# New memory for the W_o stage, a weight home that does not overlap it, and an earlier tenth weight load

## The chip, the cores and the metric

One core of one Trainium2 chip runs the whole program. The metric is the device time of one execution in microseconds. Three runs of the kernel before took 1180.64, 1182.9 and 1184.21 us; the median is 1182.9 us.

## The reference

One layer of a hybrid decoder for 512 prompt tokens and 8 sample tokens (520 rows of 1024 numbers, f32). Three gated branches (dilated attention, a state-space layer, cross-attention) are merged, multiplied by W_o and added to x. A mixture of experts follows:

```
h  = x + merged @ w_o                     # 520 x 1024
hn = rmsnorm(h, norm2)
grp_logits = hn @ w_grp + b_grp           # 4 groups, the best one
exp_logits = hn @ w_exp + b_exp           # 32 experts, the best two of the group
y  = sum over the two experts e of gate_e * ((silu(hn @ w1[e]) * (hn @ w3[e])) @ w2[e])
out = rmsnorm(h + y, norm_f)
```

Each of w1[e], w3[e] and w2[e] has 2 MB. The 96 of them are 201 MB and are read once. The change touches the stage from `h` to the first expert.

## The kernel before, in words

**Weight homes.** On-chip memory is one array, `arena`; a place in it is given in KB per partition. A weight matrix takes 16 KB per partition. `HOMES` lists ten such places. Load number n (n = 3 e + part; part 0 is w1, 1 is w3, 2 is w2 of expert e) goes to home n mod 10. The first ten loads wait only until other uses of their place are over. From load 10 on, `wait_release` waits until TensorE has used up load n - 10: semaphores `w1x` (w1), `gu` (w3), `y` (w2). So load 10 waits for expert 0's w1 product, load 15 for expert 1's w2 product. All weight loads are issued by SP, in order, into one hardware queue. SP also issues the loads of x for the W_o stage, between weight loads.

**The W_o stage.** The 520 rows are five tiles in the order `ORDER = (4, 0, 1, 2, 3)`: tile i = 0 is the 8 sample rows, tiles 1 to 4 have 128 rows each. For a tile, in the order in which its parts depend on each other:

- PE (TensorE): `out_rows(i, quarter)`, four quarters of 8 matmuls of 128x512 each (L1171). Quarters 0 and 1 make the left half of the product, 2 and 3 the right half.
- DVE (VectorE): `add_half(i, half)` adds the product onto x in `xh` (L2096).
- ACT (ScalarE): squares of the left half (L1612) and of the right half (L1619), a square root, then `hn` = x times the reciprocal, written to `hnb` (L1627).
- POOL (GpSimd): stores the tile's h rows to memory (L707, semaphore `hacc`) and then its hn rows (L709, semaphore `hnst`), both in one software queue.
- PE: `turn_half` transposes h, `router(i)` makes the logits.
- DVE: `first_squares(i)` waits for the left squares of tile i. After it in DVE's program comes `route(i - 1)`, some 20 small operations (L2129 the first, L2143 sets `chosen`) that pick the experts of the tile before, and then `add_half(i, 1)`.
- PE: `rank(i - 1)` (L1203, L1205) needs `chosen` of tile i - 1. It stands behind quarter 3 of tile i and ahead of the first quarter of tile i + 1, and each engine runs its program in order.

After the last tile PE makes the index lists (`idxmm`), DVE turns them into integers (L2190), and POOL gathers 128 rows of hn for the first two experts (L721). It waits for the lists and for all `hnst` and `hacc` stores.

**Memory of that stage, before.** `xh` has three buffers and `hnb` two; the unneeded squares go to `scrap`. W_o lies in two pieces of 16 KB, at 50 (home 6) and at 187.25 (home 8). Home 7 is where `gates`, the left operand of the product, lies. So loads 6, 7 and 8 wait for the stage's end. SP's order there is: two W_o loads, the last of norm_f's loads (`gain_f`), three x tiles, load 0; after the merge load 1; then, each time behind `hacc`, `hn` and `ht` of an earlier tile, an x tile and loads 2, 3, 4, and an x tile and load 5. Load 6 follows the last product. Load 7 is issued in two halves, one behind the `hnst` stores and one, like loads 8 and 9, behind the first gather (`xg`).

Of the kernel before, what the change touches and what calls it, by code (L numbers as in the profile page):

```python
# [32 lines left out]
P = 128  # L33
# [64 lines left out]
HOMES = (66, 107.25, 123.25, 139.25, 155.25, 171.25, 50, 91.25, 187.25, 30)  # L98
# [5 lines left out]
SPLIT = tuple(16 if i == 7 else 0 for i in range(NHOME))  # L104
# [32 lines left out]
def build(nc, t):  # L137

    with ExitStack() as ctx:
# [165 lines left out]
        scrap = [at(87, D // 2), at(89, D // 2)]  # L305
# [35 lines left out]
        hT = [at(XN + 16, 2, P), at(86, 2, P)]  # L341
        xg = at(82, D)
        gain_f = at(46, D)
# [4 lines left out]
        y_end = at(87, D // 2)  # L348
        pick_end = [at(MK + 16.25, NT, CAP), at(MK + 18.25, NT, CAP)]
        place_end = at(89, TOK)  # L350
# [22 lines left out]
        rows_in = [sem(f"s_rows_in{i}") for i in range(3)]  # L373
        hacc = [sem(f"s_hacc{i}") for i in range(3)]
        hnst = [sem(f"s_hnst{i}") for i in range(2)]

        def h_back_in(T):

            return (rows_in[T], 16 * (len(range(T, NT, 3)) + 1)) if T < 3 else \
                (kdec[T], 32 * len(range(T, NB, NSLOT)) + 16)  # L380
# [3 lines left out]
                    ssm_right=("ssmp", 16), pick=("Sfree", KT), turned=("Sj", KT), placed=("merged", KT), sums=("Pj", 2 * KT),  # L384
# [75 lines left out]
        def _(sp):  # L460
# [21 lines left out]
            def load_x(i):  # L482
                T = ORDER[i]
                src = t["x_prompt"].rearrange("(a r) c -> r a c", r=NCLS)[T] if T < 4 else t["x_sample"]
                sp.dma_start(xh[i % 3][0:ROWS[T], :], src).then_inc(rows_in[i % 3], 16)
# [86 lines left out]
            split = home(2, 1)[0]  # L572

            def load_half(k0):
                sp.dma_start(up_w[split][:, k0:k0 + KT // 2, :],
                             t["w3"][2].rearrange("(p k) f -> p k f", p=P)[:, k0:k0 + KT // 2, :]
                             ).then_inc(wld[split], 16)
# [16 lines left out]

            sp.wait_ge(s["npass"], 1)
# [21 lines left out]
        def _(pool):  # L617
# [86 lines left out]
            for i, T in enumerate(ORDER):  # L704
                n = ROWS[T]
                pool.wait_ge(s["h"], 2 * i + 2)
                pool.dma_start(h_acc[T * P:T * P + n, :], xh[i % 3][0:n, :]).then_inc(hacc[i % 3], 16)  # L707
                pool.wait_ge(s["hn"], i + 1)
                pool.dma_start(t["hn_dram"][T * P:T * P + n, :], hnb[i % 2][0:n, :]).then_inc(hnst[i % 2], 16)  # L709
            pool.wait_ge(s["xgclear"], 1)  # L710
            for i in range(2):
                pool.wait_ge(hnst[i], 16 * len(range(i, NT, 2)))
            for i in range(3):
                pool.wait_ge(hacc[i], 16 * len(range(i, NT, 3)))
# [47 lines left out]
        def _(pe):  # L762
# [404 lines left out]
            def out_rows(i, quarter):  # L1167

                T, half = ORDER[i], quarter // 2
                for k in range(4 * (quarter % 2), 4 * (quarter % 2) + 4):  # L1170
                    last = pe.matmul(bank[:, 2 * (i % 2) + half, :], gates[:, k, T * P:T * P + P],  # L1171
                                     w_o[k // 4][:, k % 4, half * 512:(half + 1) * 512],
                                     start=k == 0, stop=k == KT - 1)
                if quarter % 2 == 1:
                    last.then_inc(s["wo_mm"], 1)

            def turn_half(i, half):
                n = ROWS[ORDER[i]]
                pe.wait_ge(s["h"], 2 * i + half + 1)
                if half:  # L1180
                    pe.wait_ge(s["htA"], i + 1)
                else:
                    wait_from(pe, s["htD"], i)
                for k in range(4):
                    last = pe.transpose(bank[:, 4, k * P:k * P + n],
                                        xh[i % 3][0:n, (4 * half + k) * P:(4 * half + k + 1) * P], ident[0:n, 0:n])
                last.then_inc(s["ht"], 1)
# [30 lines left out]
            pe.wait_ge(s["wo"], 32)  # L1218
            pe.wait_ge(s["Sfree"], KT)
            for k in range(KT):  # L1220
                pe.wait_ge(s["merged"], k + 1)
                for q in range(4):
                    last = pe.matmul(bank[32 * q:32 * q + NB, 0, 0:256], gates[:, k, SEQ:TOK],
                                     w_o[k // 4][:, k % 4, q * 256:(q + 1) * 256],
                                     start=k == 0, stop=k == KT - 1, skip_group_check=True)
# [41 lines left out]
            def one_pass(p, again):  # L1267
# [30 lines left out]
                def up(e):  # L1298
                    u = e % 2
                    pe.wait_ge(s["xc"], p * NE + (2 * (e // 2) + 4))  # L1300
                    pe.wait_ge(s["hid"], p * NE + (e + 1))
                    for part, done in enumerate(("w1x", "gu")):
                        i, turn = home(e, part)
                        w = up_w[i]
                        pe.wait_ge(wld[i], p * (16 * LOADS[i]) + (16 * turn + 16 + SPLIT[i]))
# [16 lines left out]
                def down(e):  # L1322
# [6 lines left out]
                    pe.wait_ge(wld[i], p * (16 * LOADS[i]) + (16 * turn + 16 + SPLIT[i]))  # L1329
# [73 lines left out]
        def _(act):  # L1403
# [202 lines left out]
            for q in range(1, 4):  # L1606
                act.activation(hnb[0][0:NB, q * 256:(q + 1) * 256], bank[32 * q:32 * q + NB, 0, 0:256], ACT.Copy
                               ).then_inc(s["h_moved"], 1)
            for i, T in enumerate(ORDER):
                n, x = ROWS[T], xh[i % 3]  # L1610
                act.wait_ge(s["h"], 2 * i + 1)
                act.activation(scrap[0][0:n, :], x[0:n, 0:512], ACT.Square, accum_out=stat[0:n, 32 + i:33 + i]  # L1612
# [6 lines left out]
                act.activation(scrap[1][0:n, :], x[0:n, 512:D], ACT.Square, accum_out=stat[0:n, 37 + i:38 + i]  # L1619
# [6 lines left out]
                wait_from(act, hnst[i % 2], 16 * (i // 2))  # L1626
                act.activation(hnb[i % 2][0:n, :], x[0:n, :], ACT.Copy, scale=stat[0:n, 5 + i:6 + i]  # L1627
# [8 lines left out]
            act.activation(scrap[0][:, 0:1], scrap[0][:, 0:1], ACT.Silu).then_inc(s["hss"], 1)  # L1636
# [64 lines left out]
        def _(dve):  # L1701
# [388 lines left out]
            def add_half(i, half):  # L2090
                cols = slice(512 * half, 512 * half + 512)
                dve.wait_ge(s["wo_mm"], 2 * i + half)
                if half == 0:
                    dve.wait_ge(rows_in[i % 3], 16 * (i // 3 + 1))
                x = xh[i % 3][:, cols]
# [8 lines left out]
            def turned_half(i):  # L2104
# [4 lines left out]
                                bank[:, 4, :].rearrange("p (k a) -> p k a", k=4)[:, :, 0:n]).then_inc(s["htD"], 1)  # L2109
# [57 lines left out]
            TT(xh[0][0:NB, 256:D], xh[0][0:NB, 256:D], hnb[0][0:NB, 256:D], ALU.add).then_inc(s["vchain"], 1)  # L2167
# [104 lines left out]
            dve.wait_ge(hnst[1], 16 * len(range(1, NT, 2)))  # L2272
# [167 lines left out]
```

## Time and profile before

| what | value |
|---|---|
| median of three runs | 1182.9 us |
| profiled execution, its own time | 1183.2 us |
| its span (first to last instruction) | 1181.5 us |
| PE busy | 1066.9 us, 90% |
| DVE, ACT, POOL busy | 412.2, 227.1, 135.1 us |
| weight loads in the page's list of DMA issues | 95 of 2048 KB and 2 of 1024 KB |

The page cuts the span into 40 slices of 29.5 us. In slices 24 to 38 the DMA engines are 90% busy or more and move about 420 GB/s (392 in the second of them); in the five slices before, from 561 to 709 us, they move 34, 313, 169, 173 and 412 GB/s. A busy TensorE is not a TensorE at its peak; idle time counts only on the engine that others wait for.

### The profile page before, as it was taken

How to read it: one execution, taken by the hardware profiler on the slowest of the kernel's cores; microseconds unless marked ns; L12 is line 12 of the kernel's file. 1: busy time of each engine (PE TensorE's matmuls, PEld its weight loads, DVE VectorE, ACT ScalarE, POOL GpSimd, SP SyncE). 2: the span in 40 equal slices, each digit the busy share in tenths (PEclk: the TensorE clock that was granted, in tenths of full speed). 3: DMA queues.
4: the chain of work that ended last, by engine and by line, in shares of the span. 5: the costliest groups of instructions: out<-in, count | busy, mean ns of one | idle time of the engine just before them, and what ended most of it. 6: DMA issues, size and time to landing. Idle time of an engine off the chain costs nothing.

```text
span 1181.5 us, 16647 instructions
## 1 busy us (share of the span) xinstructions
PE 1066.9 (90%) x6831; PEld 761.1 (64%) x6831; DVE 412.2 (35%) x869; ACT 227.1 (19%) x445; POOL 135.1 (11%) x153
## 2 busy tenths in 40 slices
PE   7999999999999999999999599987887787888885
PEld 6888888887888888878845355544444444444441
DVE  3993305926566655422543510100000000000003
ACT  4103021125232222410032201111101111111114
POOL 2113401003010100000010011110011111110100
PEclk9999999999999999999999799999999999999998
DMA  6771266434766645279084499999999999999974
GB/s 229 248 263 55 90 226 229 136 113 169 231 227 229 219 158 188 93 280 395 34 313 169 173 412 392 415 418 420 417 418 421 420 420 421 424 421 419 418 316 148
DMA packets 50812, 330.32 MB, mean 280 GB/s; under 512 B 9084, under 2 KB 12236, under 8 KB 37552
## 3 DMA queue, kind: packets, MB, share of 16 engines
q1 hardware_dynamic: 33760, 259.75, 54.9%
q0 software_dynamic: 15104, 63.85, 16.3%
q10 hardware_dynamic: 1872, 5.66, 1.3%
q8 instruction: 53, 0.87, 0.3%
q14 instruction: 23, 0.19, 0.0%
HBM read 319.18 MB, written 62.11 MB: 323 GB/s over the span
## 4 chain that ended last, share of the span: by engine, by line
PE 64%; DMA 31%; ACT 2%; issue 1%; DVE 1%; SPq 1%; POOLq 0%; ACTq 0%; DVEq 0%
DMA arena<-in_w 26%; PE bank L777 14%; PE bank L957 12%; PE bank L1308 8%; PE bank L1171 5%; PE bank L1333 4%; PE bank L1162 4%; DMA arena<-in_w_stream 2%; PE bank L1081 2%; PE bank L869 2%; PE bank L790 1%; PE bank L948 1%; PE bank L996 1%; PE bank L1017 1%; ACT arena L1588 1%
## 5 line engine op out<-in xcount | busy, mean ns | idle before, releaser
L1308 PE MATMUL bank<-arena 128*64 128x256 f32 x2048 | 261.3, 411 | 64.9 <-DMA arena<-in_w 64.8
L1308 PEld LDWEIGHTS bank<-arena 128*64 128x64 f32 x2048 | 160.2, 143 | 157.9 <-issue 51.0
L777 PE MATMUL bank<-arena 128*128 128x260 f32 x768 | 169.8, 383 | 0.6 <-DMA arena<-in_w_stream 0.6
L777 PEld LDWEIGHTS bank<-arena 128*128 128x128 f32 x768 | 145.5, 190 | 23.3 <-issue 1.0
L957 PE MATMUL bank<-arena 128*128 128x260 f32 x672 | 152.6, 384 | 1.7 <-DVE arena L1913 1.7
L957 PEld LDWEIGHTS bank<-arena 128*128 128x128 f32 x672 | 125.7, 190 | 22.0 <-DVE arena L1913 2.5
L2244 DVE TENSOR_TENSOR arena<-arena,bank 128x256 f32<-128x256 f32 x32 | 13.5, 421 | 326.7 <-ACT arena L1645 326.7
L1333 PE MATMUL bank<-arena 128*64 128x512 f32 x512 | 117.2, 600 | 3.9 <-DVE arena L2250 3.0
L733 POOL DMA_INDIRECT y_dram<-arena,scatter_rows x31 | 44.3, 1428 | 385.6 <-ACT arena L1661 355.2
L1333 PEld LDWEIGHTS bank<-arena 128*64 128x64 f32 x512 | 37.3, 138 | 64.9 <-issue 55.6
L1645 ACT ACTIVATE arena<-bank 128x256 f32<-128x256 f32 x32 | 12.3, 383 | 318.9 <-PE bank L1308 318.9
L1661 ACT ACTIVATE arena<-bank,arena 64x512 f32<-64x512 f32 x62 | 42.3, 682 | 105.8 <-PE bank L1333 100.1
L1171 PE MATMUL bank<-arena 128*128 128x512 f32 x128 | 58.7, 601 | 0.0
L1438 ACT ACTIVATE arena<-bank 128x520 f32 (+1 forms) x24 | 14.5, 603 | 150.4 <-PE bank L777 150.4
L2236 DVE TENSOR_TENSOR arena<-bank,arena 128x512 f32<-128x512 f32 x32 | 20.6, 686 | 62.1 <-PE bank L1295 62.1
L1162 PE MATMUL bank<-arena 128*128 128x260 f32 x192 | 42.2, 382 | 0.0
L1162 PEld LDWEIGHTS bank<-arena 128*128 128x128 f32 x192 | 36.5, 190 | 5.6
L1171 PEld LDWEIGHTS bank<-arena 128*128 128x128 f32 x128 | 23.1, 190 | 23.6 <-issue 23.4
L2023 DVE TENSOR_TENSOR arena<-arena,bank 128x520 f32<-128x520 f32 x24 | 16.6, 692 | 54.7 <-PE bank L1081 26.5
L1774 DVE TENSOR_TENSOR arena<-arena 128x16 f32<-128x16 f32 (+6 forms) x24 | 13.0, 583 | 60.3 <-ACT arena L1478 59.8
L1081 PE MATMUL bank<-arena 128*128 128x260 f32 x128 | 29.7, 387 | 0.6 <-DVE arena L2023 0.6
L633 POOL DMA_DIRECT2D out_sample_swa_k<-in_cache_swa_k x24 | 14.0, 582 | 138.5 <-PE bank L777 69.5
(356 smaller groups left out, 1123.8 us busy)
## 6 DMA issues: line engine op xcount, KB each, us to landing
arena<-in_w SPq DMA_DIRECT2D x95, 2048.0 KB, 35.7
arena<-in_w_stream SPq DMA_DIRECT2D x50, 512.0 KB, 5.1
out_sample_swa_k<-in_cache_swa_k POOLq DMA_DIRECT2D x8, 2047.0 KB, 9.6
out_sample_swa_v<-in_cache_swa_v POOLq DMA_DIRECT2D x8, 2047.0 KB, 10.0
arena<-in_cache_mem_v SPq DMA_DIRECT2D x8, 512.0 KB, 8.2
arena<-in_w_o SPq DMA_DIRECT2D x2, 2048.0 KB, 9.9
out_sample_swa_k<-in_cache_swa_k POOLq DMA_DIRECT2D x8, 511.0 KB, 5.9
out_sample_swa_v<-in_cache_swa_v POOLq DMA_DIRECT2D x8, 511.0 KB, 5.7
```

What stands on the lines that cost most here:

```text
L733: pool.indirect_dma_start(out=h_acc, out_offset=bass.IndirectOffsetOnAxis(ap=rows, axis=0), in_=y_sb[e % NYS], in_offset=None, bounds_chec ...
L777: last = pe.matmul(bank[:, 2 * u + h, 0:HALF], ring[u][:, k, :], x[:, k, h * HALF:(h + 1) * HALF], start=k == 0, stop=k == KT - 1)
L869: last = pe.matmul(bank[:, 2 * u, 0:MEM], ring[u][:, k, :], memn[:, k, :], start=k == 0, stop=k == KT - 1)
L957: last = pe.matmul(bank[:, product_bank[m], 0:HALF], wq[i][left[m]][:, k, :], right[m][:, k, :], start=opens and k == 0, stop=k == 3, skip ...
L1081: last = pe.matmul(bank[:, SSM_BANK[j] + h, 0:HALF], w_ssm[k][:, j * P:(j + 1) * P], ssmT[:, k, h * HALF:(h + 1) * HALF], start=k == 0, st ...
L1162: last = pe.matmul(bank[:, 2 + 2 * i + h, 0:HALF], w[:, k, j * P:(j + 1) * P], src[:, k, h * HALF:(h + 1) * HALF], start=k == 0, stop=k == ...
L1171: last = pe.matmul(bank[:, 2 * (i % 2) + half, :], gates[:, k, T * P:T * P + P], w_o[k // 4][:, k % 4, half * 512:(half + 1) * 512], start ...
L1308: last = pe.matmul(bank[64 * q:64 * q + CAP, 2 + u, part * FE // 2:(part + 1) * FE // 2], xgT[e // 2 % 2][:, k, 64 * u:64 * u + CAP], w[:, ...
L1333: last = pe.matmul(bank[64 * q:64 * q + CAP, 6 + u, :], hT[u][:, j, par_ * CAP:(par_ + 1) * CAP], down_w[i][:, j, par_, q * 512:(q + 1) * ...
L1661: last = act.activation(y_sb[v][:, q * 512:(q + 1) * 512], bank[half, 6 + u, :], ACT.Copy, scale=slot_gate[half, e:e + 1])
L2023: return TT(g, g, bank[:, b0:b0 + 2, 0:HALF], ALU.mult)
L2236: TT(xgT[pair % 2][:, 4 * half:4 * half + 4, :], bank[:, half, :].rearrange("p (k a) -> p k a", k=4), wide(gain2_x[:, 4 * half:4 * half + ...
```

## The change

Homes 0, 6, 7 and 8 move. W_o is cut in rows of 4 KB at 38, 42, 46 and 50.25 and one piece of 16 KB at 187.25 (now home 7). Home 6 is now at 75.25 and overlaps neither W_o nor `gates`, so load 6 need not wait for the stage's end. To make room, `xh` gets two buffers instead of three and `hnb` one instead of two; `scrap` is gone, and the squares are written into `hnb`, so the left squares of tile i wait for the `hnst` store of tile i - 1. In the last tile PE takes the lower half of W_o (k 4 to 7) first, for both halves of the product; behind that load 7 is issued, and loads 8 and 9 wait for the last product, the stores and `hn`, but not for the gather. norm_f's load moves behind the last weight load.

```diff
-HOMES = (66, 107.25, 123.25, 139.25, 155.25, 171.25, 50, 91.25, 187.25, 30)
+HOMES = (59.25, 107.25, 123.25, 139.25, 155.25, 171.25, 75.25, 187.25, 91.25, 30)
...
-        w_o = [at(HOMES[6], 4, D), at(HOMES[8], 4, D)]
-        xh = [at(30 + 4 * i, D) for i in range(3)]
-        hnb = [at(42, D), at(MK + 16.25, D)]
+        w_o = [at(kb, D) for kb in (38, 42, 46, 50.25)] + [at(HOMES[7] + 4 * k, D) for k in range(4)]
+        xh = [at(30 + 4 * i, D) for i in range(2)]
+        hnb = at(MK + 16.25, D)
...
-            sp.dma_start(w_o[1], t["w_o"][:, 4:8, :]).then_inc(s["wo"], 16)
             sp.wait_ge(s["Sj"], KT)
-            sp.dma_start(w_o[0], t["w_o"][:, 0:4, :]).then_inc(s["wo"], 16)
-            sp.dma_start(gain_f, t["norm_f"].partition_broadcast(P)).then_inc(s["gainf"], 16)
-            for i in range(3):
+            for k0, n in ((0, 2), (2, 1), (3, 1), (4, 4)):
...
+                sp.dma_start(dst, src).then_inc(s["wo"], 16)
+            for i in range(2):
                 load_x(i)
             load_weight(0, 0)
             sp.wait_ge(s["merged"], KT)
             load_weight(0, 1)
-            for i in (3, 4):
-                sp.wait_ge(hacc[i % 3], 16)
-                sp.wait_ge(s["hn"], i - 2)
-                sp.wait_ge(s["ht"], 2 * (i - 2))
+            for i in range(2, NT):
+                sp.wait_ge(hacc[i % 2], 16 * (i // 2))
+                sp.wait_ge(s["hn"], i - 1)
+                sp.wait_ge(s["ht"], 2 * (i - 1))
                 load_x(i)
-                for n in ((2, 3, 4), (5,))[i - 3]:
+                for n in ((2, 3), (4, 5), (6,))[i - 2]:
                     load_weight(n // 3, n % 3)
+            sp.wait_ge(*later("wo_right", 1))
+            load_weight(2, 1)
             sp.wait_ge(s["wo_mm"], 2 * NT - 1)
-            load_weight(2, 0)
+            load_weight(2, 2)
             for i in range(2):
-                sp.wait_ge(hnst[i], 16 * len(range(i, NT, 2)))
-            load_half(0)
-            for i in range(3):
-                sp.wait_ge(hacc[i], 16 * len(range(i, NT, 3)))
+                sp.wait_ge(hacc[i], 16 * len(range(i, NT, 2)))
             sp.wait_ge(s["ht"], 2 * NT)
-            sp.wait_ge(s["xg"], 16)
-            load_half(KT // 2)
-            load_weight(2, 2)
+            sp.wait_ge(s["hn"], NT)
             load_weight(3, 0)
             for n in range(NHOME, NLOAD):
                 wait_release(n // 3, n % 3)
                 load_weight(n // 3, n % 3)
+            sp.dma_start(gain_f, t["norm_f"].partition_broadcast(P)).then_inc(s["gainf"], 16)
...
             def out_rows(i, quarter):
...
+                if i == NT - 1:
+                    half, opens, closes = quarter % 2, quarter < 2, quarter >= 2
+                    ks = range(4, 8) if opens else range(4)
...
+                elif i == NT - 1 and quarter == 1:
+                    last.then_inc(later_sem("wo_right"), 1)
...
-                turn_half(i, 0)
+                if i < NT - 1:
+                    turn_half(i, 0)
                 slot_tokens(i - 2)
                 out_rows(i, 3)
+                if i == NT - 1:
+                    turn_half(i, 0)
                 rank(i - 1)
...
                 act.wait_ge(s["h"], 2 * i + 1)
-                act.activation(scrap[0][0:n, :], x[0:n, 0:512], ACT.Square, accum_out=stat[0:n, 32 + i:33 + i]
+                wait_from(act, hnst, 16 * i)
+                act.activation(hnb[0:n, 0:512], x[0:n, 0:512], ACT.Square, accum_out=stat[0:n, 32 + i:33 + i]
                                ).then_inc(s["hss"], 1)
...
-                wait_from(act, hnst[i % 2], 16 * (i // 2))
-                act.activation(hnb[i % 2][0:n, :], x[0:n, :], ACT.Copy, scale=stat[0:n, 5 + i:6 + i]
+                act.activation(hnb[0:n, :], x[0:n, :], ACT.Copy, scale=stat[0:n, 5 + i:6 + i]
```

In the last tile the second transposition uses another bank (2 instead of 4). The weight waits of PE lose the extra count of the split load.

## Rows read from the trace of the kernel before

**Rows 1.** Chain of waits, 760 to 1181 us: start, us, what
```profile
806.41 35.70 DMA arena<-in_w
```
**Rows 2.** Waits of PE, 684 to 780 us: us in total, times, longest
```profile
PE bank L1308 <- DMA arena<-in_w: 0.6, 1, 0.6
```
**Rows 3.** Timeline of SP, 520 to 760 us: start, us, line, what, count
```profile
601.79 0.33 SPq L485 DMA_DIRECT2D arena<-in_x_prompt  x1
...
718.01 0.80 SPq L466 DMA_DIRECT2D arena<-in_w  x2
```
**Rows 4.** Timeline of SP, 687 to 688 us
```profile
687.79 0.33 SPq L466 DMA_DIRECT2D arena<-in_w  x1
```
**Rows 5.** Chain of waits, 540 to 760 us
```profile
664.40 8.44 DMA hn_dram<-arena
...
673.78 5.08 DMA arena<-hn_dram,gather_rows
```
**Rows 6.** Timeline of POOL, 586 to 684 us; in brackets the idle time before
```profile
602.01 0.52 POOL L709 DMA_DIRECT2D hn_dram<-arena  x1 [6.21 <-ACT arena L1627]
...
615.02 0.54 POOL L709 DMA_DIRECT2D hn_dram<-arena  x1 [4.69 <-ACT arena L1627]
```
**Rows 7.** DMA issues at 602, 609.8 and 615 us: KB, us to landing
```profile
hn_dram<-arena POOLq DMA_DIRECT2D x1, 32.0 KB, 4.1
...
y_dram<-arena POOLq DMA_DIRECT2D x1, 512.0 KB, 11.6
...
hn_dram<-arena POOLq DMA_DIRECT2D x1, 512.0 KB, 9.2
```
**Rows 8.** DMA issues at 632.4, 664.4 and 681.8 us
```profile
hn_dram<-arena POOLq DMA_DIRECT2D x1, 512.0 KB, 2.9
...
hn_dram<-arena POOLq DMA_DIRECT2D x1, 512.0 KB, 8.4
...
arena<-hn_dram,gather_rows POOLq DMA_INDIRECT x1, 10.3
```
**Rows 9.** DMA issues of a weight load at 602.2 and at 718.0 us
```profile
arena<-in_w SPq DMA_DIRECT2D x1, 2048.0 KB, 8.3
...
arena<-in_w SPq DMA_DIRECT2D x1, 2048.0 KB, 10.9
```
**Rows 10.** Timeline of ACT, 586 to 684 us
```profile
616.95 0.63 ACT L1612 ACTIVATE arena<-arena 128x512 f32<-128x512 f32 x1 [2.21 <-DVE arena L2096]
```
**Rows 11.** Timeline of DVE, 586 to 684 us
```profile
618.00 0.26 DVE L2129 SCALAR_TENSOR_TENSOR arena<-bank,arena 128x36 f32<-128x36 f32 x1
...
621.66 0.19 DVE L2143 TENSOR_TENSOR arena<-arena 128x32 f32<-128x32 f32 x1
...
660.73 0.69 DVE L2096 TENSOR_TENSOR arena<-arena,bank 128x512 f32<-128x512 f32 x1 [3.59 <-PE bank L1171]
...
670.36 0.38 DVE L2190 TENSOR_SCALAR gather_rows<-bank 64x16 uint32<-64x16 f32 x2 [0.74 <-PE bank L1212]
```
**Rows 12.** Timeline of PE, 586 to 684 us
```profile
608.39 0.41 PE L1205 MATMUL bank<-arena 128*128 128x32 f32 x2
...
625.81 0.39 PE L1205 MATMUL bank<-arena 128*128 128x32 f32 x2
...
652.52 3.68 PE L1171 MATMUL bank<-arena 128*128 128x512 f32 x8
```
**Rows 13.** Timeline of PE, 795 to 860 us: one wait of an expert
```profile
810.46 9.20 PE L1308 MATMUL bank<-arena 128*64 128x256 f32 x64 [3.68 <-DMA arena<-in_w]
```
**Rows 14.** Stretch of 4 us: PE, PEld, DVE, ACT, POOL busy, granted clock, DMA, GB/s
```profile
811.00:815.00 4.00, 4.00 (x24) 2.64 (x22) 0.00 (x0) 0.00 (x0) 0.00 (x0) 0.57 1.00 397
```
**Rows 15.** Page, DMA rate in 40 slices; and queues: packets, MB, share
```profile
GB/s 229 248 263 55 90 226 229 136 113 169 231 227 229 219 158 188 93 280 395 34 313 169 173 412 392 415 418 420 417 418 421 420 420 421 424 421 419 418 316 148
...
q1 hardware_dynamic: 33760, 259.75, 54.9%
q0 software_dynamic: 15104, 63.85, 16.3%
```

More of the change, by code:

```diff
@@ L103 @@
 END_BANK = (0, 2, 4, 6, 0)
-SPLIT = tuple(16 if i == 7 else 0 for i in range(NHOME))
 LATE = 29
@@ L372, in build @@
         wld = [sem(f"s_wld{i}") for i in range(NHOME)]
-        rows_in = [sem(f"s_rows_in{i}") for i in range(3)]
-        hacc = [sem(f"s_hacc{i}") for i in range(3)]
-        hnst = [sem(f"s_hnst{i}") for i in range(2)]
+        rows_in = [sem(f"s_rows_in{i}") for i in range(2)]
+        hacc = [sem(f"s_hacc{i}") for i in range(2)]
+        hnst = sem("s_hnst")
         def h_back_in(T):
-            return (rows_in[T], 16 * (len(range(T, NT, 3)) + 1)) if T < 3 else \
+            return (rows_in[T], 16 * (len(range(T, NT, 2)) + 1)) if T < 2 else \
                 (kdec[T], 32 * len(range(T, NB, NSLOT)) + 16)
@@ L706, in _ @@
                 pool.wait_ge(s["h"], 2 * i + 2)
-                pool.dma_start(h_acc[T * P:T * P + n, :], xh[i % 3][0:n, :]).then_inc(hacc[i % 3], 16)
+                pool.dma_start(h_acc[T * P:T * P + n, :], xh[i % 2][0:n, :]).then_inc(hacc[i % 2], 16)
                 pool.wait_ge(s["hn"], i + 1)
-                pool.dma_start(t["hn_dram"][T * P:T * P + n, :], hnb[i % 2][0:n, :]).then_inc(hnst[i % 2], 16)
+                pool.dma_start(t["hn_dram"][T * P:T * P + n, :], hnb[0:n, :]).then_inc(hnst, 16)
             pool.wait_ge(s["xgclear"], 1)
+            pool.wait_ge(hnst, 16 * NT)
             for i in range(2):
-                pool.wait_ge(hnst[i], 16 * len(range(i, NT, 2)))
-            for i in range(3):
-                pool.wait_ge(hacc[i], 16 * len(range(i, NT, 3)))
+                pool.wait_ge(hacc[i], 16 * len(range(i, NT, 2)))
             def one_pass(p, late=0):
@@ L1169, in out_rows @@
                 T, half = ORDER[i], quarter // 2
-                for k in range(4 * (quarter % 2), 4 * (quarter % 2) + 4):
+                ks = list(range(4 * (quarter % 2), 4 * (quarter % 2) + 4))
+                opens, closes = quarter % 2 == 0, quarter % 2 == 1
+                if i == NT - 1:
+                    half, opens, closes = quarter % 2, quarter < 2, quarter >= 2
+                    ks = range(4, 8) if opens else range(4)
+                for k in ks:
                     last = pe.matmul(bank[:, 2 * (i % 2) + half, :], gates[:, k, T * P:T * P + P],
-                                     w_o[k // 4][:, k % 4, half * 512:(half + 1) * 512],
-                                     start=k == 0, stop=k == KT - 1)
-                if quarter % 2 == 1:
+                                     w_o[k][:, half * 512:(half + 1) * 512],
+                                     start=opens and k == ks[0], stop=closes and k == ks[-1])
+                if closes:
                     last.then_inc(s["wo_mm"], 1)
+                elif i == NT - 1 and quarter == 1:
+                    last.then_inc(later_sem("wo_right"), 1)
             def turn_half(i, half):
@@ L1179, in turn_half @@
                 pe.wait_ge(s["h"], 2 * i + half + 1)
-                if half:
+                b = 2 if half and i == NT - 1 else 4
+                if half and b == 4:
                     pe.wait_ge(s["htA"], i + 1)
@@ L1184, in turn_half @@
                 for k in range(4):
-                    last = pe.transpose(bank[:, 4, k * P:k * P + n],
-                                        xh[i % 3][0:n, (4 * half + k) * P:(4 * half + k + 1) * P], ident[0:n, 0:n])
+                    last = pe.transpose(bank[:, b, k * P:k * P + n],
+                                        xh[i % 2][0:n, (4 * half + k) * P:(4 * half + k + 1) * P], ident[0:n, 0:n])
                 last.then_inc(s["ht"], 1)
@@ L1304, in up @@
                         w = up_w[i]
-                        pe.wait_ge(wld[i], p * (16 * LOADS[i]) + (16 * turn + 16 + SPLIT[i]))
+                        pe.wait_ge(wld[i], p * (16 * LOADS[i]) + (16 * turn + 16))
                         for k in range(KT):
@@ L1328, in down @@
                         pe.wait_ge(s["sgate"], p + 1)
-                    pe.wait_ge(wld[i], p * (16 * LOADS[i]) + (16 * turn + 16 + SPLIT[i]))
+                    pe.wait_ge(wld[i], p * (16 * LOADS[i]) + (16 * turn + 16))
                     for j in range(2):
@@ L1618, in _ @@
                 act.wait_ge(s["h"], 2 * i + 2)
-                act.activation(scrap[1][0:n, :], x[0:n, 512:D], ACT.Square, accum_out=stat[0:n, 37 + i:38 + i]
+                act.activation(hnb[0:n, 512:D], x[0:n, 512:D], ACT.Square, accum_out=stat[0:n, 37 + i:38 + i]
                                ).then_inc(s["hss"], 1)
@@ L1635, in _ @@
             act.wait_ge(s["hss"], 3 * NT)
-            act.activation(scrap[0][:, 0:1], scrap[0][:, 0:1], ACT.Silu).then_inc(s["hss"], 1)
+            act.activation(stat[:, 63:64], eps_ap, ACT.Silu).then_inc(s["hss"], 1)
             def one_pass(p, late=0):
@@ L2271, in _ @@
             slot_tables()
-            dve.wait_ge(hnst[1], 16 * len(range(1, NT, 2)))
+            dve.wait_ge(hnst, 16 * NT)
             for k in range(2):
```

39 lines of the change are left out of this document (18 added, 21 removed).

## The prediction

> **What bounds the kernel now.** I read the page's DMA rates first, then the chain of waits, then each engine's timeline around the W_o stage, and last the landing times of single transfers.
>
> The page shows two regimes. From some 690 us to the end of the weights the DMA rate stays close to 420 GB/s [rows 15], and the chain runs through weight transfers of some 36 us each, with short pieces of TensorE between [rows 1]. There the kernel is bound by the weight stream: what ends earlier is whatever lets the stream run earlier. Just before, it moves 34 to 313 GB/s [rows 15]: that is the room the change wants to fill, with loads 6 to 9.
>
> The reader is then to ask what releases the stream's later parts. Load 10 is issued at 687.8 [rows 4], when TensorE has finished w1 of expert 0. Load 15 is issued at 718.0 [rows 3], when expert 1's w2 product is done. In between, PE waits for weights for only 0.6 us in all [rows 2]. So from the first gather to load 15 TensorE sets the pace, not the weights. The gather is released by the last hn store (landed at 664.4 + 8.4 = 672.8) and takes 5.1 us, to 678.9 [rows 5]. Everything that moves the gather moves load 15, and from there the stream is full.
>
> **The change part by part.**
>
> *Loads 6 to 9 earlier.* Behind the first gather (678.9) now stand the second half of load 7 and loads 8 and 9. The plain count says that these two and a half vanish from the stream. But loads 10 to 14 follow TensorE's releases, and load 15 comes 30.2 us after load 10 (718.0 - 687.8). What can be gained is only the queue in front of load 15: it lands 10.9 us after its issue, a load with an idle queue in front lands after 8.3 [rows 9]. Five loads in 30 us leave the engines idle before load 15 in the new kernel. Gain 2.6 us. Bounds: nothing, if load 15 still finds a queue, and 2.6.
>
> *One hn buffer: the left squares wait for the store.* The squares of tile i now wait until the hn store of tile i - 1 has landed. Behind the squares stand `first_squares(i)`, `route(i - 1)` on DVE, and `rank(i - 1)` on PE, with tile i + 1's product behind that in PE's program. In tile 2 the squares start at 616.95 [rows 10], `route` at 618.00, its `chosen` ends at 621.85 [rows 11]. So `rank` can run 4.9 us after the squares begin; with two semaphore hops of 0.05 and 0.1 us it is 5.05 us after the landing.
>
> - Tile 0's store (32 KB) is issued at 602.0 [rows 6] and lands after 4.1 us [rows 7], because the x tile and two weight loads are issued from 601.8 on [rows 3]; SP waits there for the same `hacc`, `hn` and `ht` counts in the new kernel, so I take the same 4.1. Landing 606.1, `rank` at 611.15, where PE is ready at 608.39 [rows 12]: a stall of 2.8 us. Bounds 0 and 2.8.
> - Tile 1's store is issued at 615.02 [rows 6] and `rank(1)` runs at 625.81 [rows 12]: 10.8 us, less 5.05, leaves 5.7 us for the landing. Tile 2 repeats both 17.4 us later. A 512 KB store alone lands after 2.9 us, in both cases that the trace has [rows 8]: no stall. Beside weight loads the trace has 11.6 and 9.2 [rows 7], 8.4 beside one load, and 10.3 for a gather of the same size [rows 8]. Which applies? SP's wait for the next x tile is now `hn` of the tile just finished, which is also what POOL's store waits for: x tile 3 and loads 4 and 5 are issued within a microsecond of the store. I take 10.3, the transfer in the middle: stall 4.6. Bounds 0 (2.9) and 5.9 (11.6).
> - Tile 2's store meets x tile 4 and one load. I take 8.4, the row with one load: stall 2.7. Bounds 0 and 3.5 (9.2).
> - Tile 3's store meets load 7 only a microsecond later, and the left squares of the last tile come later too: nothing.
>
> *Clock.* After a wait of 3.7 us [rows 13] the granted clock falls to the lower level (1.2 GHz); the 4 us from 811 have a mean of 0.57 [rows 14], a loss of 4 x 0.43 = 1.7 us. The 4.6 us stall should do the same in front of out_rows(3, 0): 1.7 us. I count it once, since the other two stalls are shorter than the wait in that row. Bounds 0 and three times 1.7.
>
> *x tiles.* Two buffers make tile 2's x arrive some 3 us after 601.8, and DVE needs it at 616; the next two have as much room. Nothing; if a tile landed behind both weight loads instead of ahead of them, its add would still come in time by 2 us.
>
> *Last tile's order.* Its left half is now whole after quarter 2, at 652.52 + 3.68 = 656.2 [rows 12], instead of at 651. On DVE `add_half` (0.7), the squares and `route(3)` follow: 656.2 + 0.7 + 1.05 (squares to route, rows 10 and 11) + 3.85 + 0.5 for its two last operations = 662.3, where the right half's add now begins at 660.73 [rows 11]. So the index lists come 1.6 us later. In the kernel before they are ready at 670.74 [rows 11] and the gather starts at 673.78, 0.95 us after the store's landing [rows 5]. With loads 8 and 9 not yet, or hardly, in the queue when the last store goes out, the lists come last: 670.74 + 1.6 + 0.95 = 673.3, a gain of 0.5 us. Bounds: a loss of 1.6 (if the store lands late as well) and a gain of 1.4 (if the order costs nothing and the lists alone decide: 670.74 + 0.95 + a little).
>
> *The gather without half a load beside it.* 5.1 us now [rows 5]; a 512 KB transfer alone takes 2.9 [rows 8]. By the `hacc` landings load 9 is issued some 5 us ahead of the gather (an estimate) and is nearly through, so I take 4.1, a gain of 1.0. Bounds: a loss of 5.2 (10.3) and a gain of 2.2.
>
> *W_o in five loads, all behind `Sj`; norm_f last.* W_o is needed when PE comes out of the merge at 588, and its loads are issued before 548: hidden, by some 25 us. norm_f's 0.5 MB now follow load 95 and run beside the last scatters: 0.5 MB at 420 GB/s [rows 15] is 1.3 us; I take 0.5. Bounds 0 and 1.3.
>
> Sum: 2.8 + 4.6 + 2.7 + 1.7 - 0.5 - 1.0 - 2.6 + 0.5 = +8.2 us. Against the profiled execution's own 1183.2 us (span 1181.5 and 1.7 around it) that is 1191.4. The median of the runs shown is 1182.9, 0.3 lower, so I forecast 1191.
>
> **Rivals.**
>
> *Fair turns: the stores hardly suffer.* The weight queue's packets have 259.75 MB / 33760 = 7.7 KB, POOL's 4.2 KB [rows 15]. If each DMA engine took one packet from either queue in turn, the store would have 35% of 420 GB/s, 147 GB/s, and 0.52 MB would need 3.5 instead of 1.25 us: landing after 2.9 + 2.3 = 5.2, within the 5.7 us of room. Stalls 2 and 3 and the clock's fall go away: 1183.2 + 2.8 - 0.5 - 1.0 - 2.6 + 0.5 = 1182.4. For it: the gather of 5.1 us beside half a load. Against it: 11.6, 9.2, 8.4 and 10.3 [rows 7, 8]. Chance 0.18. The Trainium skill ("DMA: Bandwidth & Descriptors", section "Queues, rings and completion order") says that an engine goes round the queues that have work and switches at packet boundaries; by that rule, read as equal turns, the time would be this rival's. The trace bears that out for the gather only: less the 1.65 us that are not transfer (2.9 - 1.25), the 11.6 us store moved 53 GB/s, little more than a third of such a share.
>
> *The gather comes early: faster.* If the stores land as when alone (x tile and loads reach the engines after the store's packets) and tile 0's stall is lost in other slack, then the two gains at the gather have their full size: 1.4 and 2.2, with 2.6 at load 15: 1183.2 - 6.2 + 0.5 = 1177.5. It decides from a landing of 5.7 us downwards in tiles 1 and 2. For it: two rows of 2.9. Against it: those had no load in flight, and tile 0's 4.1 has the new kernel's own order of issue. Chance 0.10.
>
> *The loads simply leave the stream.* Two and a half loads of 5 us less: 1171. It would need PE to wait for weights before load 15, and it does so for 0.6 us [rows 2]. I count its chance, at most 0.02, with the faster case.
>
> *Every stall at its upper end.* 2.8 + 5.9 + 3.5, three falls of the clock (5.1), 1.3 for norm_f, nothing gained at the gather, 2.6 gained: +16.0, 1199. It is the upper end of the forecast, not a case of its own.
>
> **How the numbers follow.** A measurement of this kernel tells some 0.3% (3.5 us) from no change. Forecast (stores slowed, 1187 to 1198): 0.70. Fair turns, about 1182: 0.18. Early gather or shorter stream, under 1179.4: 0.12. The time is the forecast's, 1191. The range runs from 1181, which takes in most of the second case, to 1198: outside lie the third case and the last us of the upper end. Faster 0.12; same 0.18; slower 0.70.
>
> **What would show it.** In the profile of the changed kernel: PE waits ahead of L1205's `rank` for DVE, three times, some 3, 5 and 3 us; ACT's left squares wait for the DMA of hn; hn stores of 512 KB land after 8 us or more in tiles 1 and 2; the gather starts some 11 us later than 673.8; DMA is idle for some microseconds before load 10, and again before load 15, which lands some 8.3 us after its issue. Wrong would be: hn stores landing within 5.7 us (then the time is 1182 or less), or PE waiting for weights between the gather and load 15.

## The result, and the profile after

The changed kernel takes 1200.48 us (median of 4 runs, 1198.5 to 1201.24), the kernel before on the same chip 1182.59 us: a ratio of 1.0149, 95% interval 1.0130 to 1.0169. The forecast was 1191.0 with a range of 1181 to 1198. The direction was right, and the size about half of what was measured: 8 us against some 17. A second measurement of the changed kernel on another chip gave 1198.83 us and a ratio of 1.0140 (1.0116 to 1.0163). In the profile of the changed kernel `rank`'s matmul is L1203 (before: L1205), the W_o product L1166 (L1171), the router L1192 (L1194), the squares L1614 (L1612), the POOL stores L698 (h) and L700 (hn).

The chain of waits through the W_o stage (start, us, what). Before, the only hn store in it is the last one, at the stage's end [rows 5]:

```profile
605.69 4.27 DMA hn_dram<-arena
610.04 0.73 ACT arena L1614 x2
...
614.65 0.45 PE bank L1203 x2
615.11 5.16 PE bank L1166 x8
...
622.99 9.99 DMA hn_dram<-arena
...
637.86 0.41 PE bank L1203 x2
638.27 5.21 PE bank L1166 x8
...
646.19 9.91 DMA hn_dram<-arena
```

Three hn stores are now on the chain: each is released by the tile's own `hn`, and the next tile's squares wait for it. The timeline of PE shows what that costs (in brackets the idle time before an instruction and its releaser); for the kernel before see [rows 12]:

```profile
608.60 3.60 PE L1166 MATMUL bank<-arena 128*128 128x512 f32 x8
614.65 0.45 PE L1203 MATMUL bank<-arena 128*128 128x32 f32 x2 [2.46 <-DVEq L2145]
614.92 5.35 PE L1166 MATMUL bank<-arena 128*128 128x512 f32 x8
...
637.86 0.41 PE L1203 MATMUL bank<-arena 128*128 128x32 f32 x2 [3.93 <-DVEq L2145]
638.10 5.38 PE L1166 MATMUL bank<-arena 128*128 128x512 f32 x8
...
660.98 0.64 PE L1203 MATMUL bank<-arena 128*128 128x32 f32 x2 [3.84 <-DVEq L2145]
661.43 5.99 PE L1166 MATMUL bank<-arena 128*128 128x512 f32 x8
...
683.24 1.11 PE L1183 MATMUL bank<-arena 128*128 128x128 f32 x4 [0.76 <-DVE arena L2097]
684.14 3.46 PE L1192 MATMUL bank<-arena 128*128 128x36 f32 x16
...
700.09 1.94 PE L1296 MATMUL bank<-arena 128*128 128x128 f32 x8 [5.59 <-DMA arena<-hn_dram,gather_rows]
```

Each stall is followed by a quarter of the product that takes 5.35 to 5.99 us instead of 3.68. The granted clock (the third number from the end of a row) of four stretches says why: 3 us behind the first stall, behind the second, behind the third, and 5 us at the last tile's router (columns as in [rows 14]):

```profile
615.00:618.00 3.00, 3.00 (x5) 1.41 (x5) 0.71 (x2) 1.02 (x3) 0.56 (x1) 0.50 1.02 431
638.00:641.00 3.00, 3.00 (x6) 1.23 (x7) 0.94 (x3) 1.02 (x3) 0.53 (x1) 0.63 0.21 86
661.00:664.00 3.00, 3.00 (x5) 1.58 (x6) 1.04 (x3) 1.02 (x3) 0.53 (x1) 0.50 0.21 76
683.00:688.00 5.00, 4.76 (x28) 4.69 (x28) 1.84 (x7) 3.45 (x5) 1.06 (x2) 0.52 0.96 325
```

0.50 is the lower level, 1.2 GHz. It came after a wait of 2.46 us already, where the prediction had a fall only behind the longest. The last row is the router of the last tile at 1.2 GHz: 3.46 us instead of the 2.03 of the kernel before:

```profile
661.97 2.03 PE L1194 MATMUL bank<-arena 128*128 128x36 f32 x16
```

SP and POOL of the changed kernel show what goes out beside the slow stores (before: [rows 3] and [rows 6]):

```profile
622.75 0.33 SPq L483 DMA_DIRECT2D arena<-in_x_prompt  x1
623.12 0.43 SPq L464 DMA_DIRECT2D arena<-in_w  x1
623.60 0.43 SPq L467 DMA_DIRECT2D arena<-in_w  x1
```
```profile
622.99 0.54 POOL L700 DMA_DIRECT2D hn_dram<-arena  x1 [6.38 <-ACT arena L1628]
...
646.19 0.53 POOL L700 DMA_DIRECT2D hn_dram<-arena  x1 [6.39 <-ACT arena L1628]
...
695.58 1.09 POOL L711 DMA_INDIRECT arena<-hn_dram,gather_rows  x1 [8.42 <-issue]
```

The x tile and two weight loads go out between 0.2 us ahead of the store and 0.6 us behind it. At the next store, 646.19, they are an x tile 0.2 us ahead and one load (load 6) 0.1 us behind. The landings of the four 512 KB stores (issued at 622.99, 646.19, 670.13, 686.62) and of the gather (KB, us to landing; before: [rows 7] and [rows 8]):

```profile
hn_dram<-arena POOLq DMA_DIRECT2D x1, 512.0 KB, 10.0
hn_dram<-arena POOLq DMA_DIRECT2D x1, 512.0 KB, 9.9
hn_dram<-arena POOLq DMA_DIRECT2D x1, 512.0 KB, 3.3
hn_dram<-arena POOLq DMA_DIRECT2D x1, 512.0 KB, 5.5
arena<-hn_dram,gather_rows POOLq DMA_INDIRECT x1, 4.4
```

The first two had an x tile and loads beside them from the start. Ahead of the third nothing went out; load 7 followed it by 1.2 us (671.32).

**The difference of the two profiled executions**, before to after, is 18.1 us of span: 3.7 stand in front of the W_o product already; then 10.2 in the three stalls; 5.7 in the slow quarters behind them (5.35 + 5.38 + 5.99 - 3 x 3.68); 4.0 between there and the index lists; -1.8 from the lists to the gather's issue (1.60 against 3.42); -0.7 in the gather (4.42 against 5.08); -1.3 at expert 0, where the clock rises sooner (in the first 4 us of its w1 product the granted clock is 1.00, before 0.72); -1.8 from expert 1's w2 product to the end. The 3.7 us are not the change's: PE comes out of the merge at 592.35 here, at 589.47 in the second profile of the same kernel, and at 588.68 before. In that second profile the slow quarters cost 8.0 us instead of 5.7. The lists of the changed kernel, against those of [rows 11]:

```profile
693.98 0.38 DVE L2191 TENSOR_SCALAR gather_rows<-bank 64x16 uint32<-64x16 f32 x2 [0.75 <-PE bank L1210]
```

### The profile page after: what moved, and what is told of

It reads as the page before. It is cut to its first block, busy times and chain, and to the rows that moved or that the text cites. A ratio compares the mean times of both kernels' runs of the same rounds, so it can differ in the third digit from the quotient of the medians.

```text
span 1199.6 us, 16648 instructions
## 1 busy us (share of the span) xinstructions
PE 1077.8 (90%) x6831; PEld 766.8 (64%) x6831; DVE 412.3 (34%) x869; ACT 226.8 (19%) x445; POOL 135.0 (11%) x153
## 4 chain that ended last, share of the span: by engine, by line
PE 60%; DMA 33%; ACT 3%; DVE 3%; issue 1%; SPq 1%; POOLq 0%; ACTq 0%; DVEq 0%
DMA arena<-in_w 26%; PE bank L767 13%; PE bank L947 12%; PE bank L1309 7%; PE bank L1334 4%; PE bank L1152 4%; DMA arena<-in_w_stream 3%; PE bank L1166 3%; DMA hn_dram<-arena 2%; PE bank L1071 2%; PE bank L780 1%; PE bank L859 1%; PE bank L938 1%; PE bank L986 1%; PE bank L1007 1%
## 5 line engine op out<-in xcount | busy, mean ns | idle before, releaser
L1166 PE MATMUL bank<-arena 128*128 128x512 f32 x128 | 64.4, 650 | 0.0
L1166 PEld LDWEIGHTS bank<-arena 128*128 128x128 f32 x128 | 25.3, 208 | 27.1 <-issue 26.9
L859 PE MATMUL bank<-arena 128*128 128x256 f32 x128 | 28.9, 383 | 1.0 <-DMA arena<-in_w_stream 1.0
```

What stands on the lines that cost most here:

```text
L859: last = pe.matmul(bank[:, 2 * u, 0:MEM], ring[u][:, k, :], memn[:, k, :], start=k == 0, stop=k == KT - 1)
```

## The experiments

Each ran beside the kernel before on its chip; ratios are against that. Unless said otherwise a diff is against the changed kernel.

**The changed kernel again.**

> The changed kernel once more, on the chip of the next three runs. All theories: 1200.5 us (1198.5 to 1202), 18 us over before. Its profile tells where the first 3.7 us come from that the changed kernel's trace has already lost when the W_o product begins (592.35 against 588.68 us), ahead of all that the change touches. If they belong to the change, the product again begins at 592 us or later; if they are scatter of single transfers in the stages before, it begins anywhere from 588 to 592.

1198.83 us (1194.64 to 1201.95), ratio 1.0140 (1.0116 to 1.0163). Its stalls are 2.57, 3.92 and 3.79 us, its slow quarters 6.67, 6.27 and 6.13.

**Squares in memory of their own.** A scrap of 2 KB per partition, in two pieces of 1 KB, for the squares of either half; hn has its one memory still, and ACT waits for the store only when hn itself is written.

```diff
+        scrap = at(29, 2, 7488)[:, :, 0:256]
...
-                wait_from(act, hnst, 16 * i)
-                act.activation(hnb[0:n, 0:512], x[0:n, 0:512], ACT.Square, ...
+                act.activation(scrap[0:n], x[0:n, 0:512].rearrange(...), ACT.Square, ...
...
+                wait_from(act, hnst, 16 * i)
                 act.activation(hnb[0:n, :], x[0:n, :], ACT.Copy, ...
```

> Only the squares are moved: they go to 2 KB of their own, and the wait for the store stands ahead of the hn write instead of ahead of the left squares. Everything else is as changed: one hn buffer, two x tiles, the loads and their order. Theory A (the wait of the left squares for a slowed store, and the fall of the clock behind each stall): the three waits of rank (2.5, 3.9, 3.8 us) and the three falls (1.75, 1.8, 2.6) go away, 16.3 us: 1184 us, and some 1182 if the router of the last tile also runs at full clock. Rival B (the loads, their order and the last tile's order cost it, whatever the squares wait for): 1196 or more.

1181.6 us (1179.39 to 1185.66), ratio 0.9999 (0.9984 to 1.0015): the whole loss is gone. PE's timeline has no stall ahead of `rank` until the last tile and no slow quarter; SP and POOL show that the loads no longer meet the store:

```profile
626.81 0.39 PE L1204 MATMUL bank<-arena 128*128 128x32 f32 x2
627.04 3.68 PE L1167 MATMUL bank<-arena 128*128 128x512 f32 x8
```
```profile
618.73 0.33 SPq L484 DMA_DIRECT2D arena<-in_x_prompt  x1
```
```profile
616.03 0.54 POOL L701 DMA_DIRECT2D hn_dram<-arena  x1 [4.69 <-ACT arena L1630]
```

The waits of SP in this kernel (us in total, times, longest) name the condition that comes last:

```profile
SPq L484 <- DMA y_dram<-arena: 4.4, 2, 2.9
```

The x tile leaves 2.7 us behind the hn store now, because SP's last condition is no longer `hn` but the landing of the h store; the hn store lands after 3.9 us. In the next tile the x tile comes 1.2 us behind the store, which lands after 3.2. So everything that the change costs hangs on the squares in `hnb` and their wait for the store; what the other edits cost and bring adds up to nothing that can be measured.

**Loads behind the store.** The squares stay in `hnb`; SP waits for the store's landing before each pair of weight loads.

```diff
                 load_x(i)
+                sp.wait_ge(hnst, 16 * (i - 1))
                 for n in ((2, 3), (4, 5), (6,))[i - 2]:
```

> The changed kernel, with SP waiting for the tile's hn store before it issues the weight loads 2 and 3, 4 and 5, and 6 (the x tile still goes ahead). The left squares still wait for the store. Theory A: a 512 KB store beside one x tile lands after 3 to 5 us, within the 5.7 us of room, so the second and third stall and their falls of the clock go (3.9 + 1.8 + 3.8 + 2.6 = 12 us); tile 0's stall shrinks by 1 to 2 us: 1186 us (1184 to 1189). A theory in which the store is slow by itself, not through the loads: no change, 1200.

1184.68 us (1178.54 to 1187.81), ratio 1.0023 (1.0005 to 1.0041). In the profiled execution PE waits once ahead of the last tile, and shorter, and the quarter behind it runs at full speed. That execution is the fastest of the twelve (1178.54), so the usual one lost more than it shows:

```profile
609.05 0.41 PE L1204 MATMUL bank<-arena 128*128 128x32 f32 x2 [1.81 <-DVEq L2146]
609.30 3.68 PE L1167 MATMUL bank<-arena 128*128 128x512 f32 x8
...
626.47 0.39 PE L1204 MATMUL bank<-arena 128*128 128x32 f32 x2
```

The 512 KB stores issued at 615.69 and 633.09 land after 5.5 and 5.8 us and stall nothing: the room of 5.7 us of the prediction is about right. Other than expected, the x tile did not go ahead of these stores but 4.3 and 4.7 us behind them (619.94, 637.82), since the h store landed last of SP's conditions; the added wait then held the loads for only another 1.2 and 1.1 us. A store that is slow by itself is ruled out: with the loads held back, the wait on the memory costs its first stall and little else, 2.8 us by the medians.

**Only the first wait taken away.** The squares of tile 1 alone go to the scrap; tiles 2 to 4 wait as in the changed kernel.

```diff
-                wait_from(act, hnst, 16 * i)
+                if i != 1:
+                    wait_from(act, hnst, 16 * i)
+                places = [scrap[0:n]] * 2 if i == 1 else ...
```

> The changed kernel with one tile's squares moved: only those of tile 1 (the first of 128 rows) go to 2 KB of their own and do not wait for tile 0's store of 32 KB. Tiles 2, 3 and 4 still wait for the store of the tile before. Theory C (one chain): the first stall of 2.5 us is what makes hn the last of the three things that SP waits for, so that the loads go out with the store; without it SP waits for h's store instead, the hn store has a head start and lands after 4 us, as where no squares wait (3.9 and 3.2), and no later tile stalls: 1182 to 1185 us. Theory D (each store meets its own loads): only the first stall and its fall of the clock go, 4.3 us: 1195 to 1197.

1183.81 us (1181.02 to 1188.3), ratio 1.0009 (0.9996 to 1.0023). ACT still waits for the stores, but no longer than there is room:

```profile
622.56 0.63 ACT L1618 ACTIVATE arena<-arena 128x512 f32<-128x512 f32 x1 [4.89 <-DMA hn_dram<-arena]
...
638.46 0.63 ACT L1618 ACTIVATE arena<-arena 128x512 f32<-128x512 f32 x1 [3.39 <-DMA hn_dram<-arena]
```

The store goes out at 617.96 and lands after 4.5 us; the x tile and the loads follow 3.3 us behind it, at 621.26. So the three stalls are one chain. The first delays `hn` of tile 1 until it is SP's last condition; SP then sends its loads together with the store, the store takes 10 us, that stalls `rank` again, and again `hn` is last. Without the first 2.5 us the second and third stall don't come.

SP's other condition, the h store of tile 1, is delayed by the stall too, but its landing is not. The first row is the h store issued at 616.04 in the changed kernel, the second that of 612.71 in this run:

```profile
y_dram<-arena POOLq DMA_DIRECT2D x1, 512.0 KB, 5.3
y_dram<-arena POOLq DMA_DIRECT2D x1, 512.0 KB, 8.5
```

Both land at 621.2 to 621.3. `hn` is ready at 622.7 in the changed kernel and at 617.7 here, though the product starts there only 0.7 us later; the slow quarter stands in front of it in the chain of waits (615.11) and is a part of this delay.

**One part alone, in the kernel before.** One `hnb` with the squares in it; SP's order, three x buffers and W_o's memory are those of before (diff against it).

```diff
-        hnb = [at(42, D), at(MK + 16.25, D)]
+        hnb = [at(42, D), at(42, D)]
...
-                act.activation(scrap[0][0:n, :], x[0:n, 0:512], ACT.Square, ...
+                if i:
+                    act.wait_ge(hnst[(i - 1) % 2], 16 * ((i - 1) // 2 + 1))
+                act.activation(hnb[0][0:n, 0:512], x[0:n, 0:512], ACT.Square, ...
```

> The kernel before with one part of the change alone: the second hn buffer is the first one, the squares are written into it, and they wait for the store of the tile before; loads, x buffers, W_o's memory and the last tile's order stay as before. Theory (one hn memory with the squares in it is the cause, and its first short stall pulls the later ones after it): in the kernel before tile 0's store lands after 4.1 us, so rank(0) stalls 2.5 us or so and the clock falls (1.7); tile 1's store (9.2 beside loads) gives 3.5 and 1.7; tile 2's store goes out with no x tile and no load behind it, lands after some 3 us and gives none. 1182.5 + 2.5 + 1.7 + 3.5 + 1.7 = some 1192, two PE waits ahead of rank. Rival (the stalls need the new order of the loads and two x buffers as well): no PE wait ahead of rank over 1 us, 1182 to 1184.

1187.16 us (1184.63 to 1190.67), ratio 1.0049 (1.0033 to 1.0064): between the two expectations.

```profile
610.44 0.42 PE L1205 MATMUL bank<-arena 128*128 128x32 f32 x2 [2.22 <-DVEq L2146]
610.69 5.38 PE L1171 MATMUL bank<-arena 128*128 128x512 f32 x8
...
629.55 0.39 PE L1205 MATMUL bank<-arena 128*128 128x32 f32 x2
```

One stall and one slow quarter, 2.2 + 1.7 us, and no second one (the profiled execution, 1184.63, is the fastest of the six): the stall itself moved tile 1's store to 618.77, when two of the three loads of 602 had landed and the third, which takes some 19 us, had 3 us to go, and it landed after 4.6 us. The expected 3.5 + 1.7 for tile 1 did not come. So the memory alone costs about a third of the loss. The rest needs other parts of the change as well, by the traces SP's new order, in which the next tile's loads go out with the store; no run takes that order apart from the two x buffers and W_o's new places.

**TensorE kept busy in the stalls.** Extra matmuls of 128x512 into a bank nobody reads, behind the last quarter of a tile and ahead of `rank`; first 5, 8 and 8 of them, then 512 + 512 + 256 columns and twice 4 x 512.

```diff
+            def keep_busy(i, *widths):
+                for j, w in enumerate(widths):
+                    pe.matmul(bank[:, 2 * ((i + 1) % 2) + 1, 0:w], gates[:, 1 + j % 4, P:2 * P], w_o[0][:, 0:w],
+                              start=True, stop=True)
```

> The changed kernel, with 5, 8 and 8 matmuls of 128x512 that nobody reads put ahead of the three waits of rank (0.44 us each, 2.2 and 3.5 us), so that TensorE works through the stalls; the stalls stay as long. If the fall of the granted clock behind each stall is a cost of its own, 1.75 + 1.8 + 2.6 = 6 us go: 1194.5 us (1193 to 1196.5), and the trace shows a granted clock of 1.00 in the product of the next tile. If the half clock costs nothing on the path: 1200.5.

1201.38 us, ratio 1.0163 (1.0142 to 1.0184). The extra matmuls took twice what I had counted (eight: 7.03 us), longer than the stalls that they were to fill; the run decides nothing.

> The changed kernel with fewer matmuls that nobody reads ahead of the three waits of rank: 2.2, 3.5 and 3.5 us, a little less than the stalls (an f32 matmul of 512 columns takes 0.88 us here, twice what I had counted for the kernel with 5, 8 and 8). If the clock's fall is a cost of its own: 5 to 6 us less than the changed kernel on this chip, some 1194. If it is not on the path: no change, 1199 to 1200.

1193.22 us (1188.64 to 1196.01), ratio 1.0095 (1.0075 to 1.0116).

```profile
606.93 2.31 PE L1207 MATMUL bank<-arena 128*128 128x512 f32 x6
609.68 0.41 PE L1203 MATMUL bank<-arena 128*128 128x32 f32 x2 [0.45 <-DVEq L2153]
609.93 3.68 PE L1166 MATMUL bank<-arena 128*128 128x512 f32 x8
...
651.22 0.30 PE L1201 MATMUL bank<-arena 128*128 128x32 f32 x2
653.10 0.41 PE L1203 MATMUL bank<-arena 128*128 128x32 f32 x2 [1.58 <-DVEq L2153]
653.35 3.68 PE L1166 MATMUL bank<-arena 128*128 128x512 f32 x8
```

From the end of a quarter to `rank` it takes 2.6, 3.4 and 5.2 us, in the changed kernel 2.5, 4.1 and 4.0: in sum the gaps are no shorter. But PE is idle in them for 0.45 us, not at all, and 1.58 us, and all three quarters behind them take 3.68 us. Against 1.0140 and 1.0149 the ratio is lower by 0.0045 and 0.0054, 5.3 and 6.4 us, each with an uncertainty of some 3.5; the slow quarters of the first profile sum to 5.7. So the fall of the clock is a cost of its own, about a third of the whole. The chain of stalls does not need it: here tile 1's x tile (616.22) and store (616.32) still go out together, the store lands after 8.5 us, and the next one after 11.1.

**The early load with the old order.** The kernel with its own scrap, but the last tile in the order of before and load 7 behind the product.

```diff
-            sp.wait_ge(*later("wo_right", 1))
-            load_weight(2, 1)
             sp.wait_ge(s["wo_mm"], 2 * NT - 1)
+            load_weight(2, 1)
...
-                if i == NT - 1:
-                    half, opens, closes = quarter % 2, quarter < 2, quarter >= 2
```

> The kernel with the squares in a place of their own, and the last tile's product in the order of before (left half first); load 7 then waits for the end of the product, as load 8 does. If the new order is the cost that is left (index lists 1.4 us later, router partly at half clock): 2 us less than with the new order, some 1179.5. If the early load 7 is worth more than that, because loads 7 and 8 now go out together and hold up the last hn store and the gather: 3 to 8 us more, 1185 to 1190.

1185.66 us (1184.05 to 1186.95), ratio 1.0035 (1.0021 to 1.0049), slower than with the new order by some 4 us. Loads 7 and 8 now go out together, the second at 659.75, just ahead of the last hn store (663.13), which takes 12.7 us and holds the gather:

```profile
663.13 0.53 POOL L700 DMA_DIRECT2D hn_dram<-arena  x1 [2.16 <-ACT arena L1621]
676.73 1.09 POOL L711 DMA_INDIRECT arena<-hn_dram,gather_rows  x1 [13.07 <-DMA hn_dram<-arena]
```

With the new order load 7 goes out at 652, when half of the product is done, and only load 8 (661.22) stands ahead of the last store, which then lands after 6.0 us. Taken together with the early load 7, which this run gives up too, the order is therefore worth the 1.5 us that it costs.

**Both loads behind the first gather.** The kernel with its own scrap, loads 8 and 9 issued only when the first gather has landed.

```diff
             load_weight(2, 1)
             sp.wait_ge(s["wo_mm"], 2 * NT - 1)
-            load_weight(2, 2)
...
+            sp.wait_ge(s["xg"], 16)
+            load_weight(2, 2)
             load_weight(3, 0)
```

> The kernel with the squares in a place of their own, and loads 8 and 9 behind the first gather, so that nothing but the gather's own transfers is in flight there. If the early loads are worth nothing beyond the queue ahead of load 15 and the gather sets the start: the last hn store lands after 3 us and the gather takes 3 instead of 5 us, 2 us less than without, some 1179.5, and load 15 finds hardly any queue. If the bytes loaded early count in full: two loads of 5 us later in the stream, 1187 to 1191.

1180.09 us (1175.53 to 1184.86), ratio 0.9983 (0.9969 to 0.9996). The first gather takes 4.4 us as against 5.1 with the scrap alone, but the second gather, now beside both loads, 10.8 as against 4.1.

> The kernel with the squares in memory of their own and loads 8 and 9 behind the first gather, once more, to tell whether its 0.2% below the kernel before holds. If it holds: 1179 to 1181 and a ratio below 1 with an interval that excludes 1. If it was scatter: 1181 to 1183 and an interval that includes 1.

1180.44 us (1175.45 to 1185.01), ratio 0.9988 (0.9974 to 1.0001). The two together speak for 1 to 3 us below the kernel before; the second interval just includes no difference.

## Why the prediction fell short

**The mechanism held.** The squares wait for the hn store, `rank` waits for the squares, and the next quarter stands behind `rank`; the stores are slow where loads go out with them. Fair turns gave 5.2 us for a store beside loads; 10.0 and 9.9 were measured. The Trainium skill ("DMA: Bandwidth & Descriptors", section "Queues, rings and completion order") has each engine go round its queues packet by packet; read as equal turns, that is the rival's estimate of 1182. The trace does not agree with this reading.

Term by term, prediction against the profile (us):

| term | predicted | measured |
|---|---|---|
| stalls of `rank` 0, 1, 2 | 2.8, 4.6, 2.7 | 2.46, 3.93, 3.84 |
| fall of the clock behind them | 1.7, once | 1.67 + 1.70 + 2.31 (second profile: 8.0 in all) |
| last tile, to the gather's issue | -0.5 | 4.0 - 1.8 |
| the gather | -1.0 | -0.7 |
| expert 0, whose clock rises sooner | none | -1.3 |
| queue in front of load 15 | -2.6 | -1.8 |
| norm_f at the end | +0.5 | 0 (issued at 1128.3, long before the end) |
| sum | +8.2 | +14.4 |

The second profile has a span of 1200.3 us and its product starts 0.8 us later than before: 18.8 - 0.8 = 18.0 by the same reckoning. The medians lie 16.5 to 17.9 us above the kernel before, between the two.

**The step that failed is the clock.** "I count it once, since the other two stalls are shorter than the wait in that row": one row (3.68 us, then the lower level) was read as a threshold, and a row that shows a fall after 3.7 us says nothing of 2.5 us. The clock fell behind all three stalls, of 2.46, 3.93 and 3.84 us, for 1.67 to 2.31 us each (2.4 to 3.0 in the second profile). The term was 1.7 instead of 5.7 to 8.0: 4.0 to 6.3 us, the largest part of what the sum lacks. The bounds even held three falls, 5.1; that should have been the value. The run with TensorE kept busy shows the term by itself.

**The third stall** was taken with one load beside the store (8.4). It landed after 9.9, as the second did. That is 1.1 us. The first two stalls were 0.3 and 0.7 us shorter than predicted, so that the three sum to 10.2 against 10.1: the errors cancel, which is luck.

**The last tile** is the second term that failed: 2.2 us lost where 0.5 were to be gained. It was costed on DVE alone. The new order itself costs 1.5 us in the run with its own scrap (the transposition behind `add_half` starts 74.3 us after the merge, before 72.8), as predicted (1.6). But PE waits 1.0 and 0.8 us there, and then its last transposition and router ran at 1.2 GHz: 1.11 + 3.46 instead of 0.66 + 2.03, 1.9 us more to the lists. That makes 3.4 of the 4.0; the rest is not traced further. (With the loads behind the store the same waits left the router at 2.03 us, with the scrap it took 2.87: this fall comes in some executions.) The gain that was expected at the lists, from a store that lands in time, did come (-1.8), and was less than this loss.

**What was right for a reason that was not seen.** That SP's loads go out with the store was argued from SP's wait for `hn` alone; its wait for the landing of the h store was left out. They do so only because the first stall makes `hn` the last of SP's conditions; without it the x tile comes 1.2 to 3.3 us behind the store, which lands after 3.0 to 4.5. That the second and third stall came out was in this respect luck: they were priced as terms of their own, and they hang on the first.

**Load 15 and the stream** came out nearly as argued: load 15 lands 9.0 us after its issue instead of 10.9, and of the 2.6 us predicted 1.8 were found (in the second profile it lands after 7.9 us, and 1.0 us were found). The loads sent early did not shorten the stream beyond that. The two runs with loads 8 and 9 behind the gather bear this out, with 1180.1 and 1180.4 us. So the kernel without the loss (1181.6) is no faster than before.

## What to carry to other kernels

Before giving two writes one memory, ask what the wait between them holds up in program order on every engine behind it, and whether the delayed engine is then the last condition of a queue that sends big loads: a short first stall can so make the next ones. Price a stall of a busy TensorE with the fall of its clock unless a row shows that a wait as short had none. A transfer that others wait for should go out clear of weight loads by a few microseconds, and a few KB of scrap may be enough for it.

## What was not expected of the hardware

- A wait of 2.46 us (2.22 in the kernel before with one `hnb`) was followed by 1.2 GHz for some 3.3 us, an estimate from the 5.35 - 3.68 = 1.67 us lost at half speed; in the second profile, after 2.57 us, the loss was 2.99 us. After a wait of 1.81 us the next quarter took 3.68. Two waits of 1.0 and 0.8 us in the last tile were followed by 1.2 GHz in some executions and not in others. No run shows where the limit lies.
- A store of 512 KB on POOL's queue took 9.9 and 10.0 us where the x tile was issued 0.2 us ahead of it and one or two loads right behind. Where the x tile and the loads came 1.2 to 3.3 us behind the store, it took 3.0 to 4.5, nearly the 2.9 of a store alone. A difference of some 1.5 us in the order is worth 5 to 7. Why the store then takes so long, no run shows.
- An f32 matmul of 128x512 took 0.88 us at full clock (7.03 for eight), in the profile two entries each. A quarter of the W_o product, which the profile shows as x8, is therefore four matmuls (the loop in `out_rows` has four) and not eight.
